# Feed-forward of the first block, layer two, with gate and up by seven quarter products, and the conditioning sums in layer one

## What is computed

```python
# first block, for i in range(2)
x = x + mixer(x)                                   # attention, convolution and state space, gated
h = rmsnorm(x, norm_ffn[i])
gt, up = jnp.split(h @ w_ffn_in[i], 2, axis=-1)    # 1024 -> 2 x 2816
x = x + (jax.nn.silu(gt) * up) @ w_ffn_out[i]      # 2816 -> 1024
# after both layers
x = rmsnorm(x, norm_final)
# second block
mod = silu(c) @ w_ada + b_ada                      # 1024 -> 6 x 1024
h = rms_norm(x, pre_norm1) * (1.0 + sc1) + sh1     # sc1, sh1, ... are parts of mod
x = ...                                            # mixer, then relu-squared feed-forward 1024 -> 4096 -> 1024
```

## Time and profile before

| | us |
|---|---|
| median of 3 runs (2595.30 to 2596.52) | 2596.02 |
| the profiled execution's own time | 2594.88 |
| its span in the profile | 2593.4 |
| PE busy | 2527.2 (97%) |
| DVE busy | 1534.6 (59%) |
| POOL busy | 1232.0 (48%) |
| ACT busy | 951.3 (37%) |

### The profile page before, as it was taken

One profiled execution on the slowest core, in us unless ns is written; L12 is line 12 of the kernel. 1 busy time (PEld: TensorE's weight loads), 2 busy tenths in 40 slices (PEclk: granted clock), 3 DMA queues, 4 the chain that ended last, 5 costly groups with the idle time before them and its releaser, 6 DMA issues. The chain is left out here.

```text
span 2593.4 us, 33178 instructions
## 1 busy us (share of the span) xinstructions
PE 2527.2 (97%) x13084; PEld 2022.5 (78%) x13084; DVE 1534.6 (59%) x1870; ACT 951.3 (37%) x1349; POOL 1232.0 (48%) x891
## 2 busy tenths in 40 slices
PE   7999999999999999999999999989999999899997
PEld 6887778788887778777878888768777777688886
DVE  8984435843333787443484333479865477766665
ACT  5332543322222533344332222334335563433332
POOL 4434345444444533443545444447893234565551
PEclk9999999999999999999999999989999999899998
DMA  5222223254333412322234433232232122133321
GB/s 177 82 66 82 78 75 96 90 163 129 117 117 123 132 58 66 92 76 82 90 129 140 129 121 122 90 120 90 74 97 66 58 98 66 57 115 96 108 82 65
DMA packets 226636, 253.57 MB, mean 98 GB/s; under 512 B 9152, under 2 KB 202944, under 8 KB 226240
## 3 DMA queue, kind: packets, MB, share of 16 engines
q1 hardware_dynamic: 226176, 251.12, 31.3%
q10 hardware_dynamic: 320, 0.52, 0.1%
HBM read 246.90 MB, written 4.19 MB: 97 GB/s over the span
## 5 line engine op out<-in xcount | busy, mean ns | idle before, releaser
L221 POOL TENSOR_TENSOR sb_w_lo<-sb_raw,sb_w_hi 128x512 fp32r<-128x512 f32 x684 | 915.7, 1366 | 1045.8 <-ACT sb_w_hi L214 1043.8
L243 PE MATMUL ps<-sb_a_hi,sb_w_hi 128*128 128x512 f32 x1472 | 600.8, 408 | 21.7 <-DVE sb_w_lo L221 9.1
L244 PE MATMUL ps<-sb_a_lo,sb_w_hi 128*128 128x512 f32 x1472 | 582.9, 396 | 0.0
L245 PE MATMUL ps<-sb_a_hi,sb_w_lo 128*128 128x512 f32 x1472 | 582.6, 396 | 0.0
L214 ACT ACTIVATE sb_w_hi<-sb_raw 128x1024 fp32r<-128x1024 f32 x344 | 360.8, 1057 | 490.6 <-PE ps L245 425.9
L243 PEld LDWEIGHTS ps<-sb_a_hi,sb_w_hi 128*128 128x128 f32 x1472 | 277.0, 188 | 120.3 <-issue 36.8
L245 PEld LDWEIGHTS ps<-sb_a_hi,sb_w_lo 128*128 128x128 f32 x1472 | 276.9, 188 | 67.9
L244 PEld LDWEIGHTS ps<-sb_a_lo,sb_w_hi 128*128 128x128 f32 x1472 | 277.6, 189 | 63.9 <-issue 2.6
L243 PE MATMUL ps<-sb_b_hi,sb_w_hi 128*128 128x512 f32 x736 | 293.4, 399 | 11.4 <-DVE sb_b_lo L3085 7.4
L244 PE MATMUL ps<-sb_b_lo,sb_w_hi 128*128 128x512 f32 x736 | 291.8, 397 | 0.0
L245 PE MATMUL ps<-sb_b_hi,sb_w_lo 128*128 128x512 f32 x736 | 291.3, 396 | 0.0
(11 more groups left out here) (469 smaller groups left out, 4097.9 us busy)
## 6 DMA issues: line engine op xcount, KB each, us to landing
sb_raw<-in_w_in_dram SPq DMA_DIRECT2D x148, 512.0 KB, 3.7
sb_raw<-in_w_ffn_in_dram SPq DMA_DIRECT2D x88, 512.0 KB, 5.1
sb_ada<-in_w_ada_dram SPq DMA_DIRECT2D x48, 512.0 KB, 4.5
sb_raw<-in_w_ffn_out_dram SPq DMA_DIRECT2D x44, 512.0 KB, 3.9
sb_raw<-in_w_ff_dram SPq DMA_DIRECT2D x32, 512.0 KB, 4.2
sb_f_raw_d<-in_w_ff_dram SPq DMA_DIRECT2D x32, 512.0 KB, 3.8
sb_raw<-in_w_mix_o_dram SPq DMA_DIRECT2D x16, 512.0 KB, 3.5
sb_raw<-in_w_conv_o_dram SPq DMA_DIRECT2D x8, 512.0 KB, 3.4
```

Of the source, the lines that this page charges most:

```text
L221: ins = pool.tensor_tensor(w_lo[:, s, here], raw[:, s, here], w_hi[:, s, here].bitcast(F32), ALU.subtract)
L243: pe.matmul(out, wh, hi, start=first and i == 0, stop=False)
L244: pe.matmul(out, wh, lo, start=False, stop=False)
L245: ins = pe.matmul(out, wl, hi, start=False, stop=last and i == len(rhs) - 1)
```

## The change

`ffn1` is split in two. `ffn1_first` is layer one. It keeps the chunks as they are, and computes all of `mod`: 12 blocks of 512 columns in place of 256, in the same places of the queues, so that a block is two DMAs of 1 MB, and L1717 and L1719 are 128x512. PE has 12 sums in place of 6 and 12 transposes in place of 8 (each with four columns out), and bank 7 takes the transposes.

`ffn1_last` is layer two, without conditioning. Chunks 0 and 1 are as before. Before chunk 2 DVE and ACT make four differences of quarters of h with their hi and lo parts (`t_hi`, `t_lo`). The other nine chunks are nine rounds. In a round gate and up of a chunk are a 2x2 product of quarters, with gate and up as the two halves of the weights' columns, made by seven products of 24 matmuls with 256 columns instead of eight. Their names are M1 to M7; the weights of M5, M6, M7 and M3 are sums of quarters that DVE makes (`sums_123` and a fourth sum). The products are put together by seven additions on DVE (`mixed`). Three of the four banks go on first to tanh, gated value and hidden value (768 wide), the fourth later (256 wide). D0 and D1 are the downs of the chunk before; their weights come through a buffer of two (`raw_d`), and their rest is made by DVE (`rest_down`) instead of POOL. The nine rounds are written out, without a loop.

```diff
+ADA_W = 512
+ADA_BLOCKS = 6 * 1024 // ADA_W
...
-                for b in range(ADA_BLOCKS // 2):
+                for b in range(ADA_BLOCKS):
...
-                out = ada_sums[:, bass.ds(block * 256, 256)]
+                out = ada_sums[:, bass.ds(block * ADA_W, ADA_W)]
...
+        def ffn1_last(l, loaded, rounded, following):
...
+                        for r in range(mixes):
+                            load_down(2 * r + 2)
+                            sp.wait_ge(s_made, 4 * r + 4)
+                            sp.wait_ge(lo_pool, products * r + lo_of[M6])
+                            if r + 1 < mixes:
+                                load_pair(r + 1, 1)
+                            sp.wait_ge(lo_pool, products * r + lo_of[M7])
+                            if r + 1 < mixes:
+                                load_pair(r + 1, 0)
+                            load_down(2 * r + 3)
...
+                        for r in range(mixes):
+                            for j in (M1, M4, M2, M6, M5, M7, M3):
+                                p = piece(r, j)
+                                pool.wait_ge(piece_hi, p + 1)
...
+                            product(r, M1)
...
+                            product(r, M4)
+                            pe.wait_ge(m1_kept, r + 1)
+                            product(r, M2)
+                            pe.wait_ge(hid_lo_done, 2 * r + 2)
+                            pe.wait_ge(down_free, 2 * r + 2)
+                            down(piece(r, D0), r + 1, 2 * r, True, True)
+                            pe.wait_ge(up_free, 2 * r + 2)
+                            product(r, M6)
...
+                            product(r, M5)
+                            pe.wait_ge(mixed, 7 * r + U2)
+                            product(r, M7)
+                            if not last:
+                                pe.wait_ge(down_free, 2 * r + 3)
+                                down(piece(r, D1), r + 1, 2 * r + 1, True, True)
+                            pe.wait_ge(mixed, 7 * r + U5)
+                            product(r, M3)
+                            if last:
+                                pe.wait_ge(down_free, 2 * r + 3)
+                                down(piece(r, D1), r + 1, 2 * r + 1, True, False)
+                        pe.wait_ge(hid_lo_done, 2 * mixes + 2)
+                        pe.wait_ge(up_free, 2 * mixes + 2)
+                        down(tail, chunks - 1, 2 * mixes, True, True, first_bank=0)
+                        down(tail + 1, chunks - 1, 2 * mixes + 1, False, True, tile_done=down_tile)
...
+                            act.activation(m1, ps[:, 0, :], ACT.Copy).then_inc(m1_kept, 1)
+                            round_to(pieces * r + 11)
+                            gate_part(r, slice(0, 3), C21)
+                            hidden_part(r, slice(0, 3), 2 * r + 3)
+                            round_to(pieces * r + 13)
+                            gate_part(r, slice(3, 4), C12)
+                            hidden_part(r, slice(3, 4), 2 * r + 4)
...
+                            add_down(1)
+                            rest_down(piece(r, D0), 2 * r)
+                            sums_123(r)
...
+                            add_down(0)
+                            dve.wait_ge(piece_used, piece(r, M6) + 1)
+                            mx.done(tt(u2, m1, ps[:, 2, :], ALU.add))
+                            rest_down(piece(r, D1), 2 * r + 1)
...
+                            part(r, slice(0, 3), 2 * r + 3)
+                            hidden_rest(r + 2, 2 * r + 3, slice(0, 3))
+                            if last:
+                                for n in range(2):
+                                    rest_down(tail + n, 2 * mixes + n)
+                            dve.wait_ge(piece_used, piece(r, M3) + 1)
+                            mx.done(tt(ps[:, 3, :], u5, ps[:, 3, :], ALU.add))
+                            part(r, slice(3, 4), 2 * r + 4)
+                        hidden_rest(chunks - 1, 2 * mixes + 2, slice(3, 4))
+                        dve.wait_ge(piece_used, tail + 1)
+                        add_down(0, 0)
```

More of the change, by code:

```diff
@@ L1433, in mixer1, with ffn1_first @@
                 phase_end(mixer_sems)
-        def ffn1(l, loaded, rounded, following):
+        def ffn1_first(l, loaded, rounded, following):
             chunks, ups, per = CHUNKS1, 4, 6
@@ L1601, in _ @@
                             go_up(last, last_u + n, 0, n)
-                        pe.wait_ge(ada_kept, 2)
+                        pe.wait_ge(ada_kept, 3)
                         for at, part in enumerate(of_parts):
-                            rows = 128 if at == 0 else 64
                             for m in range(NB):
-                                c = 16 * at + rows // 32 * m
-                                ins = pe.matmul(ps[:, 6, c:c + rows // 32], part[:, m * P:(m + 1) * P],
-                                                ident[0:rows, 0:rows:32], start=True, stop=True)
+                                c = 16 * at + NB * m
+                                ins = pe.matmul(ps[:, 7, c:c + NB], part[:, m * P:(m + 1) * P], ident[:, 0:P:32],
+                                                start=True, stop=True)
                         ins.then_inc(ada_full, 1)
@@ L1648, in chunk @@
                             hidden(c, parity)
-                        def both_squares(tiles):
-                            for kt in tiles:
-                                if kt < 4:
-                                    act.wait_ge(down_free, 2 * last - 1)
-                                else:
-                                    act.wait_ge(tile_added, kt - 3)
-                                act.activation(a_hi_32[:, kt, :], x[:, kt, :], ACT.Square).then_inc(next_square, 1)
-                                act.activation(a_lo_32[:, kt, :], x[:, kt, :], ACT.Square, scale=norm_gains[:, 0, kt:kt + 1])\
-                                    .then_inc(next_square, 1)
                         act_keep_row(act, row[:, :])
@@ L1687, in _ @@
                             round_unit(act, n)
-                        if mixes:
-                            act_next(act, range(4), next_gain, a_hi, [b_hi_32[:, kt, :] for kt in range(4)], lambda kt: act.wait_ge(down_free, 2 * last - 1))
-                        else:
-                            both_squares(range(4))
+                        act_next(act, range(4), next_gain, a_hi, [b_hi_32[:, kt, :] for kt in range(4)], lambda kt: act.wait_ge(down_free, 2 * last - 1))
                         round_unit(act, total + 2)
-                        if not mixes:
-                            both_squares(range(4, KD))
                     @block.vector
```

443 lines of the change are left out of this document (401 added, 42 removed).

## The result

| | before | after |
|---|---|---|
| median (8 runs each) | 2598.35 | 2603.89 (2601.28 to 2605.89) |
| ratio, 95% interval | | 1.0023 [1.0014, 1.0032] |
| profiled execution / span | 2594.88 / 2593.4 | 2602.22 / 2600.7 |
| granted clock, mean | 0.991 | 0.985 |

What follows compares the result with a forecast made beforehand. PE, working 97% of the span, was taken to bound the kernel. Layer one +14.8, layer two -7.8 and the clock +4.5 gave +11.5 on 2594.88: 2606.4, or 2607 as median; range 2590 to 2621.

Steps and rivals of the forecast that it cites:

- Layer one's start: Chunks one and two of layer one: PE waits for later sums and weights, +4.5 and +2.3.
- the layer's end: End of layer one: the last blocks' sums finish 7.3 later, with 1.5 to spare, so PE waits +5.5 to 5.8.
- PE's own sums and transposes: End of layer one: six more sums, 1.9, and four more transposes, 0.6, cost PE +2.5.
- The rounds: Layer two's nine rounds against chunks: -17.5; the seam before the first round: +1.9.
- the loop's 31.8: Layer two's rounds: helper chain between POOL's rests for M7, summed to 31.75, longer than PE's 30.95.
- its two collisions: Layer two's rounds: DVE's fourth sum meets POOL's M5 rest, a down's rest meets M7's; about 1.1 each, 2.2.
- The tail: Last round of layer two: ACT rounds both last-down weights before the tanh, so PE waits +6.0 (3 to 7).
- The step out: Out of layer two: 5.6 us of PE work instead of 11.2 covers the chain, +5.6 (4.5 to 6.5).
- The clock: Half clock behind two new waits, at layer one's end and layer two's last downs: 2.25 each, +4.5.
- No loss of clock: Rival: both new waits come but the clock stays at 1.00, and chunk one waits 2.2, not 4.5: 2600; chance 0.22.
- Quicker transfers: Rival, SP's loads: they land faster than priced, shortening layer one's waits and letting PE set the rounds: 2590; chance 0.14.
- More collisions: Rival, layer two's rounds: DVE's 768-column rest and sums meet POOL's rests, two times 1.1 more per round: 2624; chance 0.14.

Runs made afterwards that it cites:

- the doubled sum: The changed kernel with DVE making the first weight sum of each round twice: 2613.52, ratio 1.0058.
- the addition moved: The changed kernel with DVE's addition of D1 to x ahead of the 768-column rest: 2603.13; with ACT's copy of M1 moved too: 2602.55.
- half loads: The changed kernel with each conditioning block loading only its first 256 columns, which the sums read twice: 2599.22, ratio 1.0002.
- rounds alone: Layer two in rounds as in the changed kernel, layer one as before, second half of `mod` copied from the first: 2591.12, ratio 0.9975.
- the conditioning alone: Layer one as in the changed kernel, layer two with the plain chunks of before without conditioning: 2610.57, ratio 1.0048.

## Why the prediction was right, and where it was off

The direction was right: slower, inside the range, with its parts where it had put them. The size was not: +11.5 against +7.3 in the profiled executions and +5.5 in the medians. That the total came as near as that is partly luck, since errors of both signs stand in it: layer one's waits and PE's own work there were priced 4.5 too high, the clock 2.7 too low, and 2.2 fell in code that the change doesn't touch.

- **Layer one's start**, +4.5 and +2.3, measured 2.71 + 0.23 - 0.36 and 1.12: 3.1 too much. The load was priced well, POOL came 4.1 later to chunk one (497.31 against 493.25). What failed is the step from POOL to PE: I let PE wait as long as POOL was late, and PE had 1.4 us in hand (before, POOL's first rest for chunk one ended at 496.26 and PE began on it at 497.64). At chunk two POOL came 7.5 later (534.50), PE itself by then 4.2, and it waited 1.12. A lateness off the path has to be reduced by the slack there before it counts; I had done so at the layer's end, and there 5.5 became 4.9.
- **PE's own sums and transposes**, +2.5: 1.7. I priced six more sums at 1.9, as much as the six before. They cost 0.87: the matmuls start in fours, 0.43 us apart at full clock, and where the 12 of before went as 4, 4, 2 and 2, the 24 go as six fours.
- **The rounds**, -17.5 and +1.9 ahead of them: -19.2 and +0.6. PE's 30.95 was 30.85, the loop's 31.8 was 31.53. The loop that was added up from the second block's rows is the one that runs, as the doubled sum showed. That its length came out within 0.3 is partly luck: one of its two collisions (1.1) is not in it, and its steps with the hand-overs between engines took about as much more. The place of the wait was wrong: PE waits at M5, 0.35 in most rounds, since POOL just meets M6 in time; the loss per round is 0.67. The table of waits names 2.4 of the 6.0 (3.0, of which 0.6 stands ahead of the first round): a product that it shows waiting 0.35 starts 0.5 late, counted from start to start, and shorter pauses are not in it.
- **The tail**, +6.0: 5.8 (6.1 to 6.4 in six other traces with this order), from the cause named, ACT's order, for half of it; the other half stayed when the order was changed, and which step of the chain makes it wasn't tried.
- **The step out**, +5.6: 5.57.
- **Not priced**: the 1.05 that layer two's start gains when no conditioning stands ahead on DVE.
- **The clock**, +4.5 for two places: 7.2. In layer one it cost 4.5: 1.5 behind chunk one's 2.71, which I had left out, 1.3 behind the 4.90, where the sums stand and not the dense matmuls that I had put there, and 1.7 behind the transposes, where no wait stands. In the tail it cost 2.2. Behind layer two the stretch, which I had left out too, grew from 17.1 to 23.9 us, but mostly into PE's own wait, where it costs nothing: 0.5. A further 2.9 fell in unchanged code near 1991, where the clock was 0.53 in this execution and 1.00 in that of before, and a shorter wait behind it gave 0.7 back. There the profile of before is the exception: eleven of the twelve experiments' traces have such a stretch.

"No loss of clock" is out: its clock did fall. Its milder start is what came. "Quicker transfers" is out at the ends (a block took 5.1 to 7.4 us to land) and in the rounds (a pair landed at a median of 4.5, as the earlier trace rows). Its premise that a wait of 2.5 leaves the clock alone is not safe either: behind waits of 2.6 to 2.75 at chunk one the clock fell in some traces and not in others (last section). "More collisions" did not come by itself.

The Trainium skill's page "SBUF — State Buffer", section "SBUF: two separate sides", calls the shared port pair an exclusive lock that the first of the two engines holds for its whole instruction. The trace agrees: the down's rest of 2.17 began 0.20 behind one of POOL's halves of 1.29 and lost 0.94 against its 1.23, a little less than what was left of that half, and POOL's next half took 2.28. With the addition moved, the rest of 768 columns lost 0.67.

**Open.** The profiled executions lie 3.5 (before) and 1.7 us (after) below their medians, and 2.9 us of half clock in unchanged code come and go. Single terms under 2 us rest on one execution each.

## What to carry to other kernels

When work moves into a stage that has room on average, place it by the stage's ends, not its mean: the same twelve blocks made layer one 14.9 us longer when they reached to both its ends and 2.5 in its middle. When PE's work per round shrinks, add up the longest chain of helpers that has to come round once per round, with its transfers; that chain is the new bound, and an edit that shortens one queue can lengthen the next by a collision. A long pause of PE costs its length and the clock behind it, and throwaway products bought about 1 us of the latter back in two traces here.

## What I had not expected of the hardware

- The same code of layer two ran its seven rounds in 220.72 us (after), 222.45 (half loads) and 223.45 (rounds alone). In the same order the pair loads landed at a median of 4.5, 4.8 and 4.8 us, at most 5.4, 5.8 and 6.3, and ACT stood 7.14, 7.41 and 7.56 us per round for them. Two more traces with the same rounds lie between, at 221.5 and 221.9. That fits a loop with a transfer in it; what makes the transfers slower there is open.
- The clock was at half behind a wait of only 2.71 at chunk one, though PE had been busy for 17.64 of the 19.60 us before. The length of the wait does not decide it: five more traces have the same code there. In two of them the clock fell as well (behind 2.62 and 2.75), in three it stayed at 1.00 (behind 2.61, 2.63 and 2.66; the window below is from the run with the conditioning alone). In the tail with ACT's order changed it fell behind 3.27 and 3.35, not behind 2.74 and 2.77. What tells them apart is open.
- The clock also fell where PE had no wait, behind the 24 transposes of four columns each, in six of the eleven traces that have them.
- PE shows as busy for 218.66 of 220.72 us in the seven rounds, though 4.8 of them are pauses. 2.1 of these show as idle, the rest only as a window longer than the same work elsewhere: 31.53 against 30.85 a round.

```profile
499.60:503.00 3.40, 2.13 (x8) 1.50 (x9) 3.40 (x3) 2.66 (x5) 3.33 (x3) 1.00 0.44 146
```
